# Spreading the modulation units anew over the stages of a two-block transformer kernel

## The reference, cut to what matters

```python
c_act = jax.nn.silu(c)                              # (1, 2048)
for l in range(2):
    mod = c_act @ w_mod[l] + b_mod[l]               # w_mod[l]: 2048 x 6144
    shift, scale, gate = jnp.split(mod, 3, axis=-1)
    h = rmsnorm(x, norm_gain[l]) * (1.0 + scale) + shift
    ...
    x = x + gate * (y @ w_out[l])
```

## The kernel before, in words

| stage | pieces | from us |
|---|---|---|
| attention q/k/v (first 48), b/d, first delta-rule q/k/v | 0-72 | 0 |
| z | 73-88 | 227 |
| second delta-rule q/k/v | 89-112 | 280 |
| gate b | 113-144 | 376 |
| branch b | 145-160 | 479 |
| gate a and branch a, merge | 161-208 | 526 |
| output and residual | 209-240 | 631 |
| up pieces 0 to 3 | 241-304 | 700 |
| first half-down | 305-336 | 846 |
| up pieces 4 to 7 | 337-400 | 913 |
| second half-down | 401-432 | 1072 |
| up pieces 8 to 10 | 433-480 | 1142 |
| last down | 481-504 | 1258 |
| layer 0 before its output gates / output gates / output | 505-591 / 592-623 / 624-655 | 1317 / 1585 / 1671 |
| layer 1, the same three | 656-742 / 743-774 / 775-806 | 1734 / 1993 / 2080 |

## Time and profile before

### The profile page before, as it was taken

The page is one execution under the profiler, slowest core; times in us unless marked ns, Lnnn a source line. Parts: engine busy times, 40 slices in busy tenths (PEclk is TensorE's granted clock), DMA queues, the critical chain, the costliest instruction groups (busy, mean ns, idle before and its releaser), DMA issues. The chain is left out here.

```text
span 2149.4 us, 34016 instructions
## 1 busy us (share of the span) xinstructions
PE 1943.2 (90%) x13292; PEld 1801.4 (84%) x13292; DVE 1719.3 (80%) x2200; ACT 1245.9 (58%) x1921; POOL 273.0 (13%) x182
## 2 busy tenths in 40 slices
PE   6999898999899999998998887899898979989898
PEld 5888798999897899897977875889887869978786
DVE  6776867958998988888989896687888876788787
ACT  5557736635556766554645557545566674566664
POOL 0000130230110023210000100041201002121010
PEclk8989999999999999998999988799999989999999
DMA  7775556658999776777989886676687867586786
GB/s 235 244 265 166 152 166 194 221 161 313 342 382 349 240 246 201 246 243 284 345 295 377 309 290 194 213 212 215 214 267 265 262 203 259 152 275 231 248 283 234
DMA packets 270764, 536.88 MB, mean 250 GB/s; under 512 B 31880, under 2 KB 40973, under 8 KB 269581
## 3 DMA queue, kind: packets, MB, share of 16 engines
q1 hardware_dynamic: 270317, 532.62, 73.9%
q10 hardware_dynamic: 288, 2.10, 0.2%
HBM read 532.55 MB, written 2.10 MB: 249 GB/s over the span
## 5 line engine op out<-in xcount | busy, mean ns | idle before, releaser
L150 PE MATMUL ps<-hh_r,w 128*128 128x256 f32 x3560 | 913.8, 295 | 52.9 <-DVE ring_r L1786 40.7
L1786 DVE SCALAR_TENSOR_TENSOR ring_r<-ring,w 128x1024 fp32r<-128x1024 f32 (+1 forms) x528 | 669.3, 1284 | 230.6 <-ACT w L1338 228.0
L150 PE MATMUL ps<-hlo,ring_r 128*128 128x256 f32 x3088 | 774.1, 290 | 0.0
L150 PEld LDWEIGHTS ps<-hh_r,w 128*128 128x128 f32 x3560 | 710.0, 199 | 68.8 <-DVE ring_r L1786 48.5
L1338 ACT ACTIVATE w<-ring 128x1024 fp32r<-128x1024 f32 (+1 forms) x528 | 548.2, 1055 | 291.6 <-DMA ring<-in_w_in 105.2
L150 PEld LDWEIGHTS ps<-hlo,ring_r 128*128 128x128 f32 x3088 | 613.8, 199 | 1.3 <-issue 1.0
L150 PE MATMUL ps<-w,AR_r 128*128 128x512 f32 x644 | 260.7, 405 | 10.5 <-DVE AR_r L1786 5.4
L150 PE MATMUL ps<-ring_r,AR_r 128*128 128x512 f32 x576 | 229.7, 399 | 0.0
L150 PE MATMUL ps<-hlo,AR_r 128*128 128x256 f32 x856 | 214.7, 289 | 0.0
L1786 DVE SCALAR_TENSOR_TENSOR AR_r<-AR,w 128x1024 fp32r<-128x1024 f32 x134 | 168.1, 1266 | 41.8 <-ACT w L1338 41.2
L150 PE MATMUL ps<-AR 128*128 128x64 f32 (+5 forms) x1340 | 179.8, 295 | 9.0 <-DVE AR L1782 5.6
(11 more groups left out here) (206 smaller groups left out, 2684.6 us busy)
## 6 DMA issues: line engine op xcount, KB each, us to landing
ring<-in_w_in SPq DMA_DIRECT2D x320, 512.0 KB, 4.6
ring<-in_w_mod SPq DMA_DIRECT2D x139, 512.0 KB, 5.8
ring<-in_w_up SPq DMA_DIRECT2D x116, 512.0 KB, 5.8
ring<-in_w_out SPq DMA_DIRECT2D x83, 512.0 KB, 5.3
ring<-in_w_down SPq DMA_DIRECT2D x61, 512.0 KB, 5.1
AR<-in_w_up SPq DMA_DIRECT2D x60, 512.0 KB, 5.3
AR<-in_w_in SPq DMA_DIRECT2D x49, 512.0 KB, 6.0
AR<-in_w_mod SPq DMA_DIRECT2D x47, 512.0 KB, 7.5
```

The lines of the kernel that those rows point to most:

```text
L150: return e.matmul(o, l, x, start=start, stop=stop, skip_group_check=True)
L1786: return e.scalar_tensor_tensor(o, a, s, b, op0, op1)
```

## The change

Only the places of the units change. Their order among themselves, their number and their work stay, with one exception in the order: the last block of shift and scale of layer 1 (16 units) now comes after the gates of layer 0, in layer 0's output gates and output stage.

```diff
     for blk in range(4):
-        add(t["w_out"][0], 512 * blk, 512, KT, "TM", "m", "resid", (blk,),
+        b = add(t["w_out"][0], 512 * blk, 512, KT, "TM", "m", "resid", (blk,),
             [lambda: inline("ahead")] if blk == 3 else None, fresh=blk == 0)
+        b_res = b if blk == 0 else b_res
...
-    z1, gb0, up0, up5 = (first_chunk(b) for b in (b_z1, b_gb[0], b_up[0], b_up[10]))
-    puts = spread([c for L in range(2) for b in range(4) for c in add_mod(L, b)],
-                  (24, 48), (z1, z1 + 16), (gb0 + 8, up0 - 4), (up5, marks[0] - 16))
+    z1, gb0, yb0, res0, up0 = (first_chunk(b) for b in (b_z1, b_gb[0], b_yb[0], b_res, b_up[0]))
+    early = [c for L in range(2) for b in range(4) for c in add_mod(L, b)]
+    puts = []
+    for lo, hi, n in ((24, 48, 10), (50, z1, 11), (z1, z1 + 16, 6), (z1 + 16, gb0, 11), (gb0, yb0, 14), (yb0, res0, 12),
+                      (res0, up0 - 4, 6), (up0 + 16, marks[0] - 16, 42)):
+        puts += spread(early[:n], (lo, hi))
+        early = early[n:]
     for L in range(2):
         g0 = first_chunk(b_g[L])
-        puts += spread([c for b in range(4, 6) for c in add_mod(L, b)], (marks[L] + 8, marks[L] + 18), (g0 - 40, g0 + 28))
+        gates = [c for b in range(4, 6) for c in add_mod(L, b)]
+        puts += spread(gates[:6], (marks[L] + 8, marks[L] + 18))
+        puts += spread(gates[6:], (g0 - 40, g0 + 20 if L == 0 else g0 + 28))
+        if L == 0:
+            puts += spread(early, (g0 + 20, g0 + 56))
```

## The result

The changed kernel takes 2142.22 us (median of 13 runs, 2134.08 to 2152.36) against 2156.02 us before on the same chips: a ratio of 0.9934 with a 95% interval of 0.9921 to 0.9948. The forecast was 2137.0 with a range of 2112 to 2162 and 0.6 on faster; the time is 13.8 us down, where 19 were forecast, and lies on the faster side of the forecast's own line of 2145.

A forecast was written before the change was run, and what follows sets the result against it. Bound: VectorE, busy 90 to 93% and ending last in full stages, with DMA at 0.97 in gates and merge. Gains 49.5 less costs 30.5 took 2151.2 to 2132 us; 4.8 for the median made 2137, range 2112 to 2162.

The forecast's parts named there:

- up 8 to 10: Up pieces 8 to 10, 21 to 9 units: 116 us falls to 102, -14 (bounds -8, -18).
- The gates: Gates and merge, 21 to 9 units: TensorE's busy time of 97.1 becomes the floor, -8 us (bounds -4, -13).
- the residual: Residual stage, 12 to 6 units: from 69 us, -4.5 (bounds -2 and -10).
- more comes back than summed: Rival: slow-clock stretches behind the waits in 913-1317 go as well, 25 us, giving 2112; chance 0.10.
- The block ends: TensorE's waits for the last accumulation of each 16 units: from 22.5 us in five to under 12.
- the 13 us fit into 33 idle ones: First q/k/v and z, 4 to 14 units: VectorE's idle time in 141-227 takes them, z tight, +3 us (bounds 0, +13).
- Layer-0 output: Layer-0 output stage, none to 10 units: VectorE 61 of 63 us, at 0.93 filled 66, +3 (bounds 0, +8).
- Up 0 to 3: Up pieces 0 to 3, none to 9 units: VectorE needs 142 us, at 0.93 filled 152, +6 (bounds 0, +13).
- Second q/k/v and gate b: Second q/k/v, 3 to 14 units, and gate b, 11 to 14: eleven go into the last 16 pieces, +9 us (bounds +2, +20).
- The floor: Rival: TensorE's busy time limits the relieved stages, which give 28 us against costs of 30: 2158; chance 0.14.
- The delta-rule chain: Rival: 24 units newly in q/k/v, z and gate b delay its short steps and open slow-clock stretches: 2184; chance 0.10.
- The bias tables: Rival: 18 units from piece 257 through up piece 4 last 2.32 us each beside POOL's additions: 2151; chance 0.10.

The follow-up runs named there:

- a_lend: The changed kernel with one more raw slot lent during layer 0's output stage, where only seven are left: 2142.76 us, ratio 0.9933.
- a_out_none: The changed kernel with the last block's 16 units moved from layer 0's output gates and output stage to the feed-forward: 2141.44 us, ratio 0.9931.
- a_thin_both: The changed kernel with each unit's transfer cut to 64 KB for 512 and VectorE's accumulations to 128 of 1024 elements: 2087.18 us.
- c1: The changed kernel with a lent slot in layer 0's output, no units in up 0 to 3, more in branch b and the gates: 2139.29 us.
- c4: The changed kernel with per-stage unit counts near the cheapest seen in traces, and the layer 0 handling and lent slot of c1: 2127.66 us, ratio 0.9854.
- c2: The changed kernel with unit counts set by hand per stage, none in layer 0's output stage: 2142.27 us, ratio 0.9936.
- c3: As c2, with no unit in up 0 to 3 and nine of the last block ahead of layer 0's first gate units: 2137.92 us, ratio 0.9914.
- the double cut: Units' transfers cut to 64 KB for 512 and accumulations to 128 of 1024 elements: 2087.18 us on the changed kernel, 2076.03 on the kernel before.
- a_ring6: The changed kernel with six raw slots in the ring instead of seven: 2203.72 us.

## Why the prediction was right, and where it was not

*The relieved stages.* The direction and the order of sizes held: up 4 to 7 -14.1 for -13, up 8 to 10 -18.2 for -14. The gates gave 14.1 for 8, beyond the bound of -13, and the residual 10.7 for 4.5, beyond its -10. The prediction kept TensorE's busy time of 97.1 in the gates as a floor, but busy time is longer at half clock (a 128x256 matmul is recorded at 0.41 us there and at 0.28 at full clock). In the kernel before this stage has 9.2 us of openings on TensorE (each over 0.4 us, between the starts of two matmuls) and 10.2 us at half clock: 106.4 - 9.2 - 5.1 = 92.1, and the stage after takes 92.3. Up 8 to 10 does the same: 114.6 less 15.7 and half of 13.7 is 92.1, and after it is 96.4 less 2.1 and half of 3.4, 92.6. So the floor of each was 92, and the rival "more comes back than summed" was half right: openings and slow clock went together in the relieved stages. In the whole span the time at half clock did not fall, by the trace's clock records 258.5 us before and 273.3 after; it moved to the stages that lost.

*The block ends.* TensorE's waits for the accumulator, 22.5 us in five before, are one of 4.4, under the 12 that were to show it. The same view of the kernel after:

```profile
L1795 DVE SCALAR_TENSOR_TENSOR macc<-ring,sm,macc x139: 1254/1279/2923, 92.2 to 2057.0; 128x1024 f32<-128x1024 f32 x139
...
  PE ps L150: 4.4, 1
```

The products of the gates and of the last block stand later than the list of the change says, by TensorE's records: before after pieces 576, 616, 727 and 767, with the change after 570, 607, 644, 724 and 767. So the last block's end is at 644, still in the layer-0 output stage.

A block end is not free where it waits for nothing either: its products take 1.84 us at full clock (1705.02 above). Gate b shows it cleanly. With a block end behind piece 130 it takes 112.2 to 112.5 us (after, a_lend, a_out_none, a_thin_both), with none 108.9 to 109.1 (eight kernels, with 11 or 13 units): 3.4 us, as a stretch of 3.4 us at half clock follows it there.

And moved block ends opened a wait of another kind. The one at piece 60, in the first q/k/v stage, waits for a PSUM bank that an attention step on VectorE frees (TensorE in order of time):

```profile
199.12 3.54 PE L150 MATMUL ps<-cst,macc 128*128 128x1 f32 x16 [7.58 <-DVE AR L1787]
```

In a_thin_both the same wait is 6.9 us, though the units' load is cut there:

```profile
PE ps L150 <- DVE AR L1789: 6.9, 1, 6.9
```

Before, such a wait of 4.9 us stood a piece later, ahead of a product of the convolution. In c1 it stands there again, and the block end, behind piece 64, waits for nothing (before, then c1):

```profile
198.02 3.57 PE L150 MATMUL ps<-cst,stg 128*128 128x1 f32 x16 [4.92 <-DVE AR L1778]
```

```profile
197.09 3.57 PE L150 MATMUL ps<-cst,stg 128*128 128x1 f32 x16 [4.91 <-DVE AR L1792]
...
208.72 1.84 PE L150 MATMUL ps<-cst,macc 128*128 128x1 f32 x16
```

c1 has seven units in the stage, the change nine. The two fewer are not what helps: c1 to c4 all have seven there, and with the block end behind piece 61 (c2, c3) the stage takes 99.3 and 101.0 us, behind 64 (c1, c4) 93.9 and 89.8. So "the 13 us fit into 33 idle ones" looked at the units and left the block end out; "the others went to early stages" gave it no cost. That is the mis-sized part of the +3.

*Layer-0 output: the step that failed.* The prediction filled VectorE to 0.93 and found 66 us for 63, +3 with a bound of +8. It came to +20.7. "VectorE 61 of 63" was no statement about this stage: VectorE is busy 69 of 97 and waits, behind ScalarE, for transfers that wait for a slot. The DMA share of 0.81 in the earlier trace rows looked like room. What binds in the main is the number of pieces in flight, which no busy column has. With each unit's place held and its load cut the cost stays (94.0), without the units it is gone (76.4), and a slot more or less moves it by -4.0 and +6.8. So the failed term is the +3: it priced ten units by VectorE's time, 0.3 us each, and the runs show 2.1 us each, 1.8 of them with the load cut.

*Up 0 to 3, +13.5 for +6*, just over the bound of +13. VectorE's share did not go over 0.93: it is 146.35 of 162, 0.90. The first product of the bias table waits for VectorE's chain, in the kernels before and after (TensorE in order of time):

```profile
802.59 2.25 PE L150 MATMUL ps<-AR 128*128 128x32 f32 x16 [3.04 <-DVE AR L1782]
```

```profile
801.85 3.59 PE L150 MATMUL ps<-AR 128*128 128x32 f32 x16 [8.39 <-DVE AR L1791]
```

That is 5.4 us of the 13.5. It is not VectorE's time for the units: with the load cut the wait is still 7.8 us, with no unit in the stage 3.0 (c1, c3), with two 6.1 (c4). In front of it ScalarE has run out of pieces to split, in the kernel after for 6.1 us where the longest such wait there before is 2.2:

```profile
791.89 1.06 ACT L1347 ACTIVATE w<-ring 128x1024 fp32r<-128x1024 f32 x1 [6.08 <-DMA ring<-in_w_up]
```

Until shortly before, SP was issuing the small transfers of the bias tables. From their start on ScalarE had five weight pieces left to split, with the load cut also five, before the change seven. That the units had taken the slots of the others is the likely reason and was not tested by itself. With the load cut the stage takes 146.1, so about half of the cost is load. The products behind piece 304 stand ahead of the first half-down's first matmul, so their 1.8 us are in this stage too. The rest stays open.

*Second q/k/v and gate b, +13.7 for +9*: inside the bounds. Of the 10.1 us in the former 6.3 are load, as the double cut leaves 82.8 of 89.1 us; of the 3.6 in gate b nearly none is (112.2 us with the cuts), it is the block end at 130. *First half-down, -0.2 for +5.5*: six units fit into it entirely, and the block end at piece 304 waited for nothing.

*The rivals.* The floor did not hold, since relieved stages got shorter by 72 us. The delta-rule chain would have cost over 31 us in the q/k/v stages, z and gate b; they took 20.3. Its slow stretches did come in part: the time at half clock in the second q/k/v stage went from 13.7 to 23.9 us. The bias tables would have made each unit there last 2.32 us; they last 1.46 (windows of up 0 to 3 and of the first half-down, units alone, columns as in the earlier trace rows without TensorE's):

```profile
689.00:851.00 162.00, 13.13 (x9) 0.93 0.70 234
851.00:917.00 66.00, 8.76 (x6) 1.00 0.83 287
```

1.46 rather than 1.26 is a price, 3 us over fifteen units. The 2.32 us of the earlier trace rows had stood beside POOL's additions of 2.3 us in the merge, not beside the bias tables. Beside two of the tables' additions, of 2.8 us each, two of the fifteen lasted 2.91 and 2.92 us, the longest of the whole trace; each began 1.0 us after the addition and ended 1.1 us after its end. The Trainium skill (SBUF — State Buffer, Who interferes with whom) calls the ports that the two engines share an exclusive lock, so that the later instruction waits. The 2.92 us agree with it; few units meet an addition, since POOL is busy only 22 of the 162 us.

*Two signs that did not show.* VectorE was to be under 0.85 in 1072-1258's stages; it is 0.92 and 0.91, because the stages got shorter along with its work. DMA was to be near 0.85 in the gates; it is 0.99 at 360 GB/s, for the same reason. A share is a ratio, and both of its terms move.

## What to carry to other kernels

Read, besides how busy each engine is, how many transfers can be in flight and how long each holds its slot: in a stage that turned over seven slots at one transfer each 2.0 us, an added transfer cost 2.1 us at full size and 1.8 at an eighth of it, even with DMA at 0.8 and the engines at 0.75. Where two resources are both full, cut both in one experiment before calling either harmless, since each alone gave 3.5 and 5.5 us here and both together 13.8. And when movable work comes in blocks with a product at the end, place the ends first: the few microseconds behind a block end in a bad place can cost more than the units around it (the first q/k/v stage: 99 to 103 us with the block end behind piece 60 or 61, 90 to 94 behind 64, with seven units in the kernels from either side).

## What the runs showed that was not expected

- Many stages cut by TensorE's own pieces repeat from kernel to kernel within a few tenths of a microsecond, while the whole time spreads over some 18 us between executions (2134.08 to 2152.36). One trace of each kernel is enough for a ledger of those stages, though the total needs many runs. The exceptions are the first q/k/v stage (100.0, 100.4, 102.9 and 101.7 in four kernels with the same places of its units), layer 1's output (66.9 to 69.4 without a unit) and the layers' first stages (layer 0's 257.1, 257.5 and 253.4 after, in a_out_none and in a_lend, with the same units there).
- The second half-down takes 59.6 us with five units and no block end among its pieces (after) and 62.0 with six and none either (c2). With the same six units and a block end that waits for nothing it takes 63.8 (c3, c4): 1.8 us for the block end. With seven units and a block end that waits 4.3 us for its accumulation it takes 69.0 (c1), with eight and no such wait 66.4 (a_out_none), and 70.9 before, with 14.
- One raw slot of seven is worth 61.5 us of 2142 (a_ring6), more than any placement of units tried here gave.
- The double cut of the kernel before takes 164 us off VectorE's busy time (1719.3 to 1555.6) and 88 MB off the transfers (532.55 to 444.47 MB read) and gives 80 us: half of VectorE's time for these units already lay beside other work.
